# A hybrid decoder layer on one core: fewer dense and more fetched tokens in the expert stage, a fixed row rate in its loop, pages behind scores, the last gates straight from their buffer

## The reference, cut to what matters

```python
def peer_block(x, w_pq, sub_keys, expert_u, expert_v):       # 8 heads, 2 x 128 keys, 16,384 experts
    q = jnp.einsum('nd,de->ne', x, w_pq).reshape(n, PEER_HEADS, 2, PEER_DQ // 2)
    s = jnp.einsum('nhpc,hpkc->nhpk', q, sub_keys)
    sv, si = lax.top_k(s, PEER_TOPK)                         # 16 best of 128 keys, twice
    cand = (sv[:, :, 0, :, None] + sv[:, :, 1, None, :]).reshape(n, PEER_HEADS, 256)
    cv, ci = lax.top_k(cand, PEER_TOPK)                      # 16 best sums: 16 experts a head
    ...
    g = jax.nn.softmax(cv, axis=-1)
    act = jax.nn.gelu(jnp.einsum('nhkd,nd->nhk', expert_u[experts], x))
    return jnp.einsum('nhk,nhkd->nd', g * act, expert_v[experts])
```

## Time and profile before

| | |
|---|---|
| median of 3 runs | 2139.24 us (2136.78 to 2145.38) |
| the profiled execution, its own time | 2147.01 us |
| span of its profile | 2145.1 us |
| mean granted TensorE clock | 0.904 |
| TensorE busy | 1915.8 us (89%) |
| VectorE busy | 1436.1 us (67%) |
| ScalarE busy | 609.1 us (28%) |
| GpSimd busy | 586.6 us (27%) |
| moved by DMA | 479.29 MB, mean 223 GB/s |

### The profile page before, as it was taken

How to read it: one execution, slowest core, us unless ns; L and a number is a source line. 1 busy time by engine, 2 the same in 40 slices (tenths; PEclk the granted TensorE clock), 3 DMA queues, 4 the chain that set the end, 5 groups by cost and what they waited for, 6 DMA issues and landing times.

```text
span 2145.1 us, 26500 instructions
## 1 busy us (share of the span) xinstructions
PE 1915.8 (89%) x9117; PEld 1500.0 (70%) x9117; DVE 1436.1 (67%) x3189; ACT 609.1 (28%) x1020; POOL 586.6 (27%) x454
## 2 busy tenths in 40 slices
PE   6988899666688988999886999999999999999994
PEld 3556674554467745667675788888888888888883
DVE  4025366243346755999986778888888777777777
ACT  1132122210011111114455333333333333333331
POOL 0000002344423123310000114454454444444440
PEclk9989999666675679999998999999999999999997
DMA  6611334354534456554438878999998888888872
GB/s 250 228 40 40 123 118 162 108 164 146 186 137 147 148 171 229 202 178 149 164 141 302 295 278 321 356 349 340 364 340 301 317 289 291 320 287 292 318 255 92
DMA packets 152645, 479.29 MB, mean 223 GB/s; under 512 B 14624, under 2 KB 75856, under 8 KB 130928
## 3 DMA queue, kind: packets, MB, share of 16 engines
q1 hardware_dynamic: 94704, 270.60, 34.8%
q0 software_dynamic: 57856, 207.65, 27.2%
HBM read 443.73 MB, written 33.94 MB: 223 GB/s over the span
## 4 chain that ended last, share of the span: by engine, by line
PE 73%; DVE 16%; another core or an unknown queue 4%; DMA 3%; issue 2%; ACT 2%; POOL 0%; SPq 0%; DVEq 0%; ACTq 0%
PE ps L1034 24%; PE ps L1024 19%; PE ps L634 6%; PE ps L970 3%; PE ps L935 3%; PE ps L986 3%; DVE lo L1650 2%; PE ps L1011 2%; PE ps L721 2%; PE ps L720 2%; PE ps L803 2%; PE ps L743 1%; PE ps L638 1%; DMA lo<-x 1%
## 5 line engine op out<-in xcount | busy, mean ns | idle before, releaser
L1478 POOL DMA_INDIRECT lo<-ur,lo x192 | 244.3, 1272 | 797.8 <-DVE lo L2011 323.5
L1478 POOL DMA_INDIRECT lo<-vr,lo x192 | 278.1, 1448 | 650.1 <-DVE lo L2079 306.7
L1024 PE MATMUL ps<-xh,uh 128*128 128x352 f32 x832 | 270.6, 325 | 0.0
L1024 PE MATMUL ps<-xh,ul 128*128 128x352 f32 x832 | 270.5, 325 | 0.0
L1024 PE MATMUL ps<-xl,uh 128*128 128x352 f32 x832 | 268.8, 323 | 0.0
L1129 ACT ACTIVATE hi<-ps 128x512 f32<-128x512 f32 (+10 forms) x259 | 154.3, 645 | 373.7 <-PE ps L970 111.9
L1034 PE MATMUL ps<-vh,hh 128*128 128x512 f32 (+1 forms) x768 | 240.9, 395 | 19.9 <-DVE vl L2047 19.9
L1034 PE MATMUL ps<-vl,hh 128*128 128x512 f32 (+1 forms) x768 | 241.1, 395 | 0.0
L1034 PE MATMUL ps<-vh,hl 128*128 128x512 f32 (+1 forms) x768 | 240.0, 394 | 0.0
L2071 DVE SCALAR_TENSOR_TENSOR lo<-lo 128x1024 f32<-128x1024 f32 x174 | 221.8, 1282 | 18.5 <-DMA lo<-vr,lo 9.7
L2047 DVE TENSOR_TENSOR vl<-hi,vh 128x1024 fp32r<-128x1024 f32 x128 | 156.9, 1226 | 48.8 <-ACT vh L1129 48.3
(11 more groups left out here) (385 smaller groups left out, 2928.5 us busy)
## 6 DMA issues: line engine op xcount, KB each, us to landing
hi<-ev SPq DMA_DIRECT2D x64, 1024.0 KB
hi<-wts SPq DMA_DIRECT2D x22, 2048.0 KB, 7.8
hi<-eu SPq DMA_DIRECT2D x38, 1024.0 KB, 10.0
lo<-eu SPq DMA_DIRECT2D x26, 1024.0 KB
gates<-hi SPq DMA_DIRECT2D x11, 2048.0 KB, 7.2
hi<-gates SPq DMA_DIRECT2D x32, 704.0 KB, 8.5
lo<-cache SPq DMA_DIRECT2D x48, 128.0 KB
hi<-cache SPq DMA_DIRECT2D x48, 128.0 KB
```

The lines of the kernel that those rows point to most:

```text
L1024: last = nc.tensor.matmul(ps[:, 6 + p, 0:GW[1]], a[p][:, k * 128:(k + 1) * 128], b[:, k, :], start=(k == 0 and b is xh and a is uh), stop= ...
L1478: nc.gpsimd.indirect_dma_start(ring[n % RING], None, table, bass.IndirectOffsetOnAxis(idxs[:, i, k:k + 1], 0)).then_inc(r_in[n % RING], 16)
```

## The change

- Tile 0 has 112 rows (96 prompt tokens and the meta tokens), tile 2 has 64: group 1 is 320 columns wide, group 0 is 240.
- Of tile 0's 96 prompt tokens the first 64 are fetched as before. The other 32 (`NV`) are written four times, 32 partitions and two heads each, into a tile of their own, `xq` (called `QUARTERS`): 32 slots more. `FSETS` = (96, 128), 448 gathers in all. They get key scores, best keys and a choice of their own.
- In "down", tile 2's low and high parts of the hidden values stand side by side (`hx`), so one product with 128 rows takes the place of two with 64 against vh: 16 products a block. The upper half of the result is copied out and added by two products with an identity after the last block.
- Rows: 128 dots ahead of the loop (6 a sample), 24 adds in the down-only blocks, one in each. In the loop six rounds with 16 dots and 8 adds, three with 16 adds to tile 1 and 8 to `xq`, three with 24 adds to tile 1: 24 rows in each of twelve rounds. The last has 8 adds and, after its fourth, fifth and sixth block, the merges and norms of tile 0, of `xq` and of tile 1.
- The pages of sample b + 2 are asked for when, besides, the scores of sample b + 1 are done (`sm_s`), on SP and on GpSimd, there after three rows.
- The gate table has 10 chunks. The gates of the first eight blocks are loaded for chunks 0 to 8 when these are stored; VectorE copies the last chunk's from its buffer. vl of block 0 comes ahead.
- The buffers are laid out anew for this.

The core of the diff:

```diff
-R = (80, 128, 96, 128, 128)
-T = (0, 80, 208, 304, 432)
+R = (112, 128, 64, 128, 128)
+T = (0, 112, 240, 304, 432)
...
-GW = (208, 352)
-LAST = (63, 127, 95, 127, 127)
+G0 = (0, 240)
+GW = (240, 320)
...
+NV = 32
...
-FSETS = (NF, SLOTS)
+FSETS = (NF + NV, SLOTS)
...
-LATE = 18
+LATE = 16
 SP_PAGES = 12
-ITER = LATE * 4 // 3
-U_SAMPLE = 5
-U_OLD = 11
+ITER = LATE * 3 // 2
+U_QUERY = 0
+U_SAMPLE = 6
+U_OLD = 16
 U_TILE = 4
-U_OUT = 15
-U_KEYS = 24
-U_PRE = SB * U_SAMPLE + U_OLD + 3 * U_TILE + U_OUT + U_KEYS
-U_LOOP = 5
+U_OUT = 20
+U_KEYS = 32
+U_PRE = U_QUERY + SB * U_SAMPLE + U_OLD + 3 * U_TILE + U_OUT + U_KEYS
+U_LOOP = 6
+V_LOOP = 3
 HS = 24
 HS_GAP = 9
 HS_TURN = 2
-V_EARLY = 6 * HS // 8
+V_EARLY = HS
...
+        hx = [rounded(f"hx{p}", SK0 + p * (LOW + GW[1]), LOW + GW[1])[:, :] for p in range(2)]
+        hh = [hx[p][:, LOW:LOW + GW[1]] for p in range(2)]
+        hl = [rounded(f"hl{p}", SK0 + 2 * (LOW + GW[1]) + p * (GW[1] - LOW), GW[1] - LOW)[:, :] for p in range(2)]
...
+        FINAL = (0, QUARTERS, 1, 3, 4, 2)
+        LN_AT = (3, 4, 5)
...
+                    for c in range(4):
+                        sp.dma_start(xq[c * NV:(c + 1) * NV, :], hid[NF:NF + NV, 0, :]).then_inc(s["dup_in"], 16)
+                    sp.wait_ge(s["dup_in"], 64)
...
                 sp.wait_ge(s["sm_o"], b - 1)
+                sp.wait_ge(s["sm_s"], b)
                 load_pages(b, rows)
...
+                if c == NCH - 1:
+                    for n in range(2):
+                        sp.wait_ge(gs_in[n], stored(n, NCH - 1))
+                    for quad in range(2):
+                        load_first_gates(quad)
...
-            for q in range(2):
-                load_gates(q, q)
...
+                if q == 0:
+                    sp.wait_ge(s["f_done"], 2 * sum(FSETS) - 8)
+                    sp.dma_start(halves[0:NF, :], hid[NF:128, 0, :]).then_inc(s["acc_in"], 16)
+                    for c in range(3):
+                        sp.dma_start(quarters[c][0:NV, :], xq[(c + 1) * NV:(c + 2) * NV, :]).then_inc(s["acc_in"], 16)
...
+                    o = NV * (hp // 4)
+                    nc.tensor.matmul(ps[o:o + NV, bank, 2 * NK:3 * NK], pqT[:, b % 2, NF:NF + NV], skT[:, hp, :], start=True, stop=True,
+                                     tile_position=(0, o))
...
-                    for a, b in ((hh, vh), (hh, vl), (hl, vh)):
+                    r, c = R[i], local(i)
+                    if i == ST:
+                        products = ((slice(0, 2 * r), hx[p][:, 0:2 * r], vh), (slice(0, r), hh[p][:, c], vl))
+                    else:
+                        low = hl[p][:, c.start - LOW:c.stop - LOW]
+                        products = ((slice(0, r), hh[p][:, c], vh), (slice(0, r), hh[p][:, c], vl), (slice(0, r), low, vh))
+                    for n, (m, a, b) in enumerate(products):
                         for half in range(2):
-                            last = nc.tensor.matmul(ps[0:R[i], 2 * slot(i) + half, :], a[p][:, local(i)],
-                                                    b[p][:, half * 512:(half + 1) * 512],
-                                                    start=(first and a is hh and b is vh), stop=(final and a is hl),
+                            last = nc.tensor.matmul(ps[m, 2 * slot(i) + half, :], a, b[p][:, half * 512:(half + 1) * 512],
+                                                    start=(first and n == 0), stop=(final and n == len(products) - 1),
                                                     skip_group_check=True)
...
+            pe.wait_ge(s["yh_done"], 1)
+            r = R[ST]
+            for half in range(2):
+                last = nc.tensor.matmul(ps[0:r, half, :], ident[r:2 * r, r:2 * r], yhigh[r:2 * r, half, :], start=False, stop=True,
+                                        skip_group_check=True)
+            last.then_inc(s["y_ps"], 1)
...
+            softmax_exp(QUARTERS, 2)
...
+            act.wait_ge(s["y_ps"], NK)
+            r = R[ST]
+            copy(yhigh[r:2 * r], ps[r:2 * r, 0:2, :]).then_inc(s["yh_done"], 1)
...
-                u_fetches(at, at + 2)
+                u_fetches(at, at + 3)
                 if b + 2 < SB:
                     pool.wait_ge(s["sm_o"], b + 1)
+                    pool.wait_ge(s["sm_s"], b + 2)
                     load_pages(b + 2)
-                u_fetches(at + 2, at + U_SAMPLE)
+                u_fetches(at + 3, at + U_SAMPLE)
...
+                v.tensor_tensor(hx[p][:, 0:LOW], ab[:, p, 0:LOW], as32(hh[p][:, 0:LOW]), ALU.subtract)
+                v.tensor_tensor(hl[p], ab[:, p, LOW:GW[1]], as32(hh[p][:, LOW:GW[1]]), ALU.subtract).then_inc(s["hl_done"], 1)
...
+                    for u in range(2):
+                        late_dot(j, n, 2 * q + u)
                         n += 1
-                        if k % 3 == 2:
-                            add_rows(j, ITER, U_AT, n, 0, j * (LATE // 3) + (V_EARLY + k // 3), None if first and k == 2 else last)
-                            n += 1
-                            last = n
+                    add_rows(j, n, acc, 0, j * 8 + (V_EARLY + q), done)
+                    n += 1
+                    done = n
...
+                    if final and q == LN_AT[0]:
+                        dve.wait_ge(s["ln2_in"], 16)
+                        dve.wait_ge(s["acc_in"], 64)
+                        step(v.tensor_tensor(hid[0:NF, 0, :], hid[0:NF, 0, :], halves[0:NF, :], ALU.add))
+                        layer_norm(hid[:, 0, :], 0, 2 * TI)
+                    if final and q == LN_AT[1]:
+                        for part in quarters:
+                            step(v.tensor_tensor(xq[0:NV, :], xq[0:NV, :], part[0:NV, :], ALU.add))
+                        layer_norm(xq, TI, 2 * TI + 1)
+                    if final and q == LN_AT[2]:
+                        dve.wait_ge(s["f_done"], 2 * NU)
+                        layer_norm(hid[:, 1, :], 1, 2 * TI + 2)
...
+            best_keys(QUARTERS, 0)
             choose(0)
+            choose(QUARTERS)
             choose(1)
...
             dve.wait_ge(s["gm_ps"], GW[1] // 4)
+            low_v((0, 0), 1)
+            fetched_gates(0)
+            dve.wait_ge(gs_in[1], stored(1, NCH))
+            dve.wait_ge(s["ev_done"], GW[1] // 4)
+            for quad in range(2):
+                ins = v.tensor_copy(gt[quad][:, NCH - 1], stage[staged(NCH - 1)][:, quad * 4:quad * 4 + 4, :])
+            step(ins)
             early_gated(0)
             low_hidden(0, 1)
...
+                early_add(b)
+            with dve.Fori(0, (NF - V_EARLY) // 8) as j:
+                eight_dots(j, hid[:, 0, :])
+            for j in range((NF - V_EARLY) // 8, U_LOOP):
+                eight_dots(j, xq)
             dve.wait_ge(s["f_done"], U_AT + ITER * U_LOOP)
             v.tensor_scalar(hid[:, 1, :], hid[:, 1, :], ALPHA, None, ALU.mult).then_inc(s["dots_done"], 1)
             fetched_gates(1)
-            eight_adds(U_LOOP, first=True)
-            with dve.Fori(U_LOOP + 1, (NK - HS) // 8 - 1) as j:
-                eight_adds(j)
-            eight_adds((NK - HS) // 8 - 1, final=True)
-
-            dve.wait_ge(s["f_done"], 2 * NU)
-            dve.wait_ge(s["ln2_in"], 16)
-            layer_norm(hid[:, 1, :], 1, 2 * TI)
-            dve.wait_ge(s["y_ps"], NK)
-            for n, i in enumerate(GROUPS[1]):
+            last, each = (NK - HS) // 8 - 1, ITER // 8
+            with dve.Fori(U_LOOP, U_LOOP + V_LOOP) as j:
+                eight_adds(j, -LATE * U_LOOP, 2, low=V_EARLY)
+            with dve.Fori(U_LOOP + V_LOOP, last) as j:
+                eight_adds(j, LATE * V_LOOP - ITER * (U_LOOP + V_LOOP), each)
+            eight_adds(last, SLOTS - 8 - 16 * last, 2, final=True)
...
+            for n, i in enumerate(FINAL[3:]):
                 r = R[i]
+                dve.wait_ge(s["y_ps"], NK + (i == ST))
```

245 lines of the change are left out of this document (136 added, 109 removed).

## The result

| | before | changed |
|---|---|---|
| median of 4 runs | 2138.37 us | 2086.76 us (2084.17 to 2093.75) |
| profiled execution, span | 2145.1 us | 2087.2 us |
| mean granted TensorE clock | 0.904 | 0.890 |

The ratio is 0.9758, 95% interval 0.9724 to 0.9791: faster by 52 us where 117 were forecast, and outside the range, whose upper end was 2080. The experiments show that the size depends on the chip: on two further chips of this kind the kernel before took 2145 and 2143 us, on three others 2079 to 2081 us. There the change gives 0.9919 (0.9892 to 0.9945), 16 us.

A forecast was written before the change was run, and what follows sets the result against it. TensorE was taken as the bound, with DMA right behind it. Terms of -76, 0, -34, +6, +7, +13, -12, -10 and -11 summed to -117 us: 2030, or 2022 in terms of the median, whole range 1993 to 2080.

The forecast's parts named there:

- rival 5: Down products and last round: stacking or the norms moved there do less than forecast, each under 8 us; inside the range.
- Rival 1: Main loop: DMA becomes the bound in twelve rounds, +32 to +42 us, 2054 to 2064 us; chance 0.17.
- -34: Sample stage: pages asked for behind the scores, with added dots and late rows counted; ends -51 and +15 us.
- 13.6 less 5.1 is 8.5 us a sample, 6 x 8.5 = -51: Samples: if loads hold the scores, each 13.6 us wait shrinks to the last sample's 5.1 us.
- rival 2: Samples: the wait only moves, so -34 becomes up to +15 us, 2056 to 2071 us; chance 0.15.
- rows behind the pages come late, some 1.3 us a sample, +8: Samples: GpSimd's 8 page gathers and 6 rows take 17.5 us of a 22 us period, delaying rows.
- the 17 us that I had put down for dots and rows: Samples: +9 us for one more dot in each of eight samples, +8 us for late rows.
- a third of ten more dots: Old states and output stage: five more dots each at 1.16 us, a third counted within the +13 us term.
- The 7 us given back: Group 1's keys: 256 key queries, 32 columns less at 0.85 ns, set against group 0's +12.6 us.
- the term for dots: 18 more dots before the loop outside the samples: +13 us (+4 to +21), 9.3 of it in the keys stage.
- The first stays: End of the gate table: the 13.48 us wait for a store to free the buffer was taken to remain.
- the other products of the first group grow by as much as the second's shrink: Groups 0 and 1 outside the keys: growth and shrinkage cancel, leaving the keys term net +6 us (0 to +13).

The follow-up runs named there:

- Pages alone: Kernel before with only its page requests moved behind the scores: 2111.36 us against 2143.30 on a chip with the waits; 2082.97 and 2086.11 on chips without.
- rows_first: Changed kernel with GpSimd asking for all six rows of a sample ahead of the pages: 2065.23 us, 0.9630 against the kernel before.
- dots_hollow: Changed kernel with its 26 extra dots ahead of the loop replaced by one-column copies, rows still fetched: 2044.11 us against 2064.38 on the same chip.

## Why the prediction was wrong, point by point

**The blocks: right, a little better.** Forecast 7.32 us, measured 7.19: all 104 blocks start 7.19 us behind each other (8.06 before). With the two down-only products that the row holds, 104 x 3.53 + 106 x 3.66 is 755 us of its 763.7, and TensorE stands still in it for 6.7:

```profile
PE ps L1086 <- DVE vl L2129: 6.7, 2, 4.9
```

Both times are in the last two blocks (4.9 and 1.8 us), behind the norms that the change put into the last round; before, TensorE didn't stand still there at all. The forecast had 17 us of norms filled in beside 12 freed and let the slack cover the rest. That is rival 5, small as forecast: the -10.7 us behind the loop cost up to 6.7 in it. Rival 1 didn't take place. ACT waits for u and the last chain goes through row transfers late in the loop, but all of it is covered, as the even 7.19 us show:

```profile
ACT uh L1186 <- DMA lo<-eu: 24.9, 18, 2.3
```

```profile
1835.94 12.82 DMA lo<-vr,lo
```

The DMA engines are full (share 1.00 to 1.03), at 386 to 402 GB/s and not at the 363 GB/s that I had made the lower end, nor at the 358 GB/s of the rule that I had put beside it (the Trainium skill, DMA: Bandwidth & Descriptors, Specifications). Whole windows of 64 us above 385 GB/s contradict that rule for this core, and agree with what the Trainium skill (HBM Reference, Specifications) says of a core that streams alone.

**Down-only blocks, direct gates, end: right.** +3.8, -12.9 and -10.7 us, forecast 0, -10 and -11, the last with the 6.7 us above against it.

**Samples: the mechanism right where there is one, the size too large.** -34 was forecast; the stage of the changed kernel came out 19.2 and, in the second profile, 32.7 us shorter. The term that was mis-sized is "13.6 less 5.1 is 8.5 us a sample, 6 x 8.5 = -51". It took the scores for 5.1 us once the loads are out of their way. Pages alone gave 26 us of stage (32 of time), since the scores of six samples then took 7.1 to 11.1 us and unnamed waits stood elsewhere in the sample: rival 2 in part. By medians undoing the condition cost 26 to 34 us, by ratios 21 to 30. The term "rows behind the pages come late, some 1.3 us a sample, +8" was low too: six bursts took 9.8 to 14.3 us instead of 7.0, 28 us of row waits in all, and rows_first gave back 14 us and more, though not by the row waits alone as far as is shown. What I hadn't thought of at all is that the gap might stand on some chips alone. Where it doesn't, the condition costs 3 to 7 us, the stage of the changed kernel is 14 to 16 us longer than before (170.6), near the 17 us that I had put down for dots and rows, and the whole change is worth 16. The two windows of the kernel before for the same stretches as above:

```profile
395.00:625.00 230.00, 158.23 (x900) 120.49 (x899) 95.61 (x252) 23.37 (x63) 101.76 (x95) 0.69 0.49 157
625.00:770.00 145.00, 129.61 (x550) 102.39 (x550) 93.13 (x316) 28.87 (x74) 26.81 (x24) 0.60 0.43 145
```

TensorE was busy 158 of 230 us in the samples and is busy 192 of 211 now, with the clock at 0.64. The first VectorE instruction on a sample's scores now waits for TensorE:

```profile
DVE lo L1947 <- PE ps L829: 34.5, 8, 8.7
```

That TensorE at half clock is the next bound, and keeps the stage near 185 us even with all rows in time, fits its 172 busy of 187 us in rows_first (116 of them low), but no run tests it.

**The mixer behind the samples: +16.8 for +4.** The sum had counted a third of ten more dots in the old states and the output stage, and took the rest for unchanged. 20 us more of it ran at 1.2 GHz than before (143 against 123 over the four parts, the mean of the first three falling from 0.60 to 0.57). The step that failed is "unchanged": the part from the last new state to the output stage took 67.6 us with 59 at the low clock, for 57.7 with 35, though it has as many products; in three other executions of the changed kernel it took 60.4 to 61.0. In the old states, +4.1, TensorE waits for a burst of 16 dots, 24.5 us long; in the kernel before for 11 dots, 16.5 us. Whether the longer burst brings about the low clock behind it stays open. The new states take 48.6 to 50.8 us in all six profiles with the old dots and 53.3 to 58.3 in all fourteen with the new ones, up to all of them at the low clock. dots_hollow has 58.2 us as well, but it doesn't test the length: its burst is still 23.7 us long, as the rows of the hollow dots are waited for.

**Group 1's keys: +7.8 for +2.** The 7 us given back came: TensorE is busy 72.9 us with the expert queries for 80.8. The key scores take 17.1 for 13.2. And the first query starts 21.7 us behind the last output product for 11.3, since its tokens' norms stand on VectorE among five bursts of dots that took 31.1 us for 17.6, one of them 11.7 us for four dots, with 6.7 us of waiting for rows. In dots_hollow that start is at 14.4 us. The step that failed is counting a third of the output stage's dots, and no waits for their rows.

**Choices and gates: +13.2 for -12, the largest miss.** VectorE comes to its last dot 17.4 us later behind TensorE's last keys: three bursts at 37.4 us instead of 21. Of that I had 7 us in the term for dots; the other 9.5 are waits for rows, which the forecast didn't have. That a burst longer than the ring waits was to be read from six slots and eight dots. From there to its last one-hots it took 223.5 us before and 218.7 after, 5 us less and not 12. The 8 fewer groups did give their 10 us: without the last tile it is 183.7 us before and 173.4 after. But the last tile's 32 groups took 45.3 us for 39.8, as ACT waits longer for a buffer of the gate table to be stored, and TensorE and VectorE (6.4 us) behind it:

```profile
ACT hi L1186 <- DMA gates<-hi: 8.4, 1, 8.4
```

```profile
1176.40 15.17 DMA gates<-hi
```

Before, that wait of ACT's was 4.0 us in the same place, the piece of the chain 13.48, and VectorE waited 0.9 us in all. The step that failed is "The first stays": this wait for a store grew, and took back half of what the groups gave. No run changes the store, so its price is read from the trace alone.

**Group 0 and the choice: +25.6 for +20.** The keys came as calculated, 12.5 us. Two more things: "the other products of the first group grow by as much as the second's shrink" was wrong, as the projections of group 1 take 20.9 us for 48 products before (at 302 us) and after (at 343 us), so only the growth, 3.5 us, is there; and the choice cost 7.5 us of wait as forecast and 2 more (6.0 in all on the chips without the waits).

In short: the loop came as forecast. Ahead of it the forecast counted the whole of a wait with no named releaser as gained (51 us; 26 came), priced added dots at VectorE's time without their rows, which each had to be fetched through six slots and one queue, and left a wait for a store and the low clock where they were.

## What to carry to other kernels

The price for one more fetched row holds, besides VectorE's time, the time from freeing its slot to its landing whenever more rows are used in a row than there are slots, and what stands in the issuing engine's queue ahead of it. Before a wait with no named releaser is priced, see whether it stands on another chip: three of the six chips here didn't have it. And when such a wait is gone from its row, compare the whole stage with a chip that never had it: here 30 us were still there, under other names. When work is moved into the last round of a full loop, look at the last blocks for what it pushes back.

## What the runs showed of the hardware

- Two kinds of chips under the same kernel: six waits of 13.6 us at score products that run while twelve page loads of 128 KB and eight gathers are asked for (2138 to 2145 us on three occasions), or none (2079 to 2081 us on three). The other stretches of the two profiles of the kernel before agree within 2.2 us, except the old states behind the samples (36.5 and 30.0 us, and both lengths occur on either kind of chip). Asked for later, the loads leave 204 us of sample stage on the one kind and 172 to 175 on the other.
- A single core moved 386 to 402 GB/s over windows of 64 us, and TensorE started a block every 7.19 us throughout.
- 358 us of the changed kernel's first 843 us ran at a granted clock of 0.5, and stretches of equal instructions (the new states) took 48.6 us with 38.3 of them low and 58.2 us with all of them low.
